# A sublayer's first products take the high part of input tile 0 alone, and the fillers of TensorE are seven at every sublayer

## The reference, cut to what matters

```python
for i in range(DEPTH):
    gn = norm_gains[i]
    h = h + 0.5 * rmsnorm(swiglu(rmsnorm(h, gn[0]), ffn1_w_in[i], ffn1_w_out[i]), gn[1])
    hn = rmsnorm(h, gn[2])
    ...                                  # m = the mixer of this layer on hn
    h = h + rmsnorm(m, gn[3])
    h = h + 0.5 * rmsnorm(swiglu(rmsnorm(h, gn[4]), ffn2_w_in[i], ffn2_w_out[i]), gn[5])
```

## Time and profile before

| | |
|---|---|
| median of 3 executions | 3162.06 us |
| the three executions | 3161.1, 3162.06, 3168.82 us |
| profiled execution, own time | 3175.51 us |
| its span, first to last instruction | 3173.4 us |
| granted TensorE clock, mean over the span | 0.996 |
| PE busy | 3125.5 us, 98% |
| DVE busy | 2176.7 us, 69% |
| ACT busy | 1666.1 us, 53% |
| DMA engines, mean share | 46.8%, 168 GB/s from HBM |

### The profile page before, as it was taken

One profiled execution on the slowest core, in us unless ns is written; L12 is line 12 of the kernel. 1 busy time (PEld: TensorE's weight loads), 2 busy tenths in 40 slices (PEclk: granted clock), 3 DMA queues, 4 the chain that ended last, 5 costly groups with the idle time before them and its releaser, 6 DMA issues.

```text
span 3173.4 us, 44497 instructions
## 1 busy us (share of the span) xinstructions
PE 3125.5 (98%) x17972; PEld 2719.3 (86%) x17972; DVE 2176.7 (69%) x2640; ACT 1666.1 (53%) x2064; POOL 4.0 (0%) x22
## 2 busy tenths in 40 slices
PE   9999999999999999999999999999999999999998
PEld 8888888888888888888888888888788888888887
DVE  7767675867586775675866777585874675857674
ACT  6565654645454654454546565454532554646553
POOL 0000000000000000000000000000000000000000
PEclk9999999999999999999999999999999999999999
DMA  6543454554355454455454345455432454554453
GB/s 231 186 172 130 151 186 173 186 187 158 120 186 186 173 186 172 147 186 186 173 186 170 123 159 186 166 193 187 149 143 107 156 186 163 199 186 149 151 191 120
DMA packets 75355, 534.77 MB, mean 169 GB/s; under 512 B 8480, under 2 KB 8608, under 8 KB 10784
## 3 DMA queue, kind: packets, MB, share of 16 engines
q1 hardware_dynamic: 75168, 532.07, 46.8%
HBM read 530.99 MB, written 1.05 MB: 168 GB/s over the span
## 4 chain that ended last, share of the span: by engine, by line
PE 93%; DVE 3%; ACT 1%; DVEq 1%; issue 1%; DMA 0%; SPq 0%; ACTq 0%
PE pp L2003 37%; PE pp L2004 18%; PE pm L2003 8%; PE pp L2153 5%; PE pm L2004 4%; PE pp L2026 4%; PE pp L2056 3%; PE pp L1998 2%; PE pp L1997 2%; PE pp L1999 2%; PE pp L2028 2%; PE pp L2196 1%; PE pm L1016 0%; PE pm L1029 0%; PE pp L373 0%
## 5 line engine op out<-in xcount | busy, mean ns | idle before, releaser
L2003 PE MATMUL pp<-xs,whi 128*128 128x512 f32 x4592 | 1628.8, 400 | 7.3 <-DVE tsum L1851 6.9
L1771 DVE TENSOR_TENSOR wlo<-raw,whi 128x2048 fp32r<-128x2048 f32 x453 | 1036.0, 2290 | 422.2 <-ACT whi L1575 421.7
L2004 PE MATMUL pp<-xs,wlo 128*128 128x256 f32 x4592 | 1288.6, 281 | 0.0
L2003 PEld LDWEIGHTS pp<-xs,whi 128*128 128x128 f32 x4592 | 864.3, 188 | 225.0 <-DVE tsum L1851 15.8
L1575 ACT ACTIVATE whi<-raw 128x2048 fp32r<-128x2048 f32 x453 | 864.3, 1911 | 281.8 <-DMA raw<-weights 280.8
L2004 PEld LDWEIGHTS pp<-xs,wlo 128*128 128x128 f32 x4592 | 869.7, 189 | 0.7
L1665 ACT ACTIVATE corr<-pp 128x512 f32<-128x512 f32 x335 | 199.3, 595 | 653.2 <-PE pp L2004 627.3
L1851 DVE TENSOR_TENSOR tsum<-pp,corr 128x512 f32<-128x512 f32 x323 | 222.8, 690 | 251.8 <-ACT corr L1665 251.6
L2003 PE MATMUL pm<-hs,whi 128*128 128x512 f32 x1056 | 377.3, 398 | 0.0
L2004 PE MATMUL pm<-hs,wlo 128*128 128x256 f32 x1056 | 297.0, 281 | 0.0
L2003 PEld LDWEIGHTS pm<-hs,whi 128*128 128x128 f32 x1056 | 199.1, 189 | 45.1
(11 more groups left out here) (346 smaller groups left out, 3133.6 us busy)
## 6 DMA issues: line engine op xcount, KB each, us to landing
raw<-weights SPq DMA_DIRECT2D x503, 1024.0 KB, 4.8
raw<-weights SPq DMA_DIRECT2D x8, 256.0 KB, 7.2
h<-x_by_feature SPq DMA_DIRECT2D x4, 256.0 KB, 6.7
out<-h SPq DMA_DIRECT2D x4, 256.0 KB, 2.5
vec<-vectors SPq DMA_DIRECT2D x1, 264.0 KB, 2.8
lamrow<-diff_lambda SPq DMA_DIRECT2D x1, 128.0 KB, 11.5
skiprow<-ssm_d SPq DMA_DIRECT2D x1, 8.0 KB, 12.3
```

Of the source, the lines that this page charges most:

```text
L1771: v.tensor_tensor(wlo[:, slot, :], raw[:, slot, :], whi[:, slot, :].bitcast(F32), ALU.subtract).then_inc(sem("weights_lo"), 1)
L2003: mm(bank, whi[:, slot, c:c + P], x_k, start=start, stop=False)
L2004: return mm(bank[:, 0:T], wlo[:, slot, c:c + P], x_k[:, 0:T], start=False, stop=stop)
```

## The change

`hi_of_tile_0` now posts a semaphore of its own, `x_hi_first`. In `rows`, tile 0 waits for that one, issues the four `wlo` products and then four `whi` products on the high part alone (256 columns each); only then it waits for the low part and issues four `whi` products on the low part alone (256 columns each, into the second half of the bank). The flag that opens the accumulation (`start`) moves to the `wlo` products of tile 0. Tiles 1 to 7 keep their order: `wlo` on the high part, then `whi` on both at once. The fillers are 7 ahead of every sublayer, where they were 5 ahead of all but the first.

```diff
             def hi_of_tile_0(s):
-                v.tensor_scalar(xs[:, 0, 0:T], h[:, 0, :], vec[:, 0, s["gain"]:s["gain"] + 1], None, ALU.mult)
+                v.tensor_scalar(xs[:, 0, 0:T], h[:, 0, :], vec[:, 0, s["gain"]:s["gain"] + 1], None, ALU.mult
+                                ).then_inc(sem("x_hi_first"), 1)
                 dve.drain()
...
                 def rows(k, outputs):
 
-                    for part in ("whi", "wlo") if k == 0 else ("wlo", "whi"):
-                        if part == "whi":
-                            pe.wait_ge(sem("x_lo"), KD * fill + k + 1)
-                        elif k:
-                            pe.wait_ge(sem("x_hi"), (KD - 1) * fill + k)
+
+
+                    if k:
+                        pe.wait_ge(sem("x_hi"), (KD - 1) * fill + k)
+                    else:
+                        pe.wait_ge(sem("x_hi_first"), fill + 1)
+                    for w in (wlo, whi) if k == 0 else (wlo,):
                         for half, ft in outputs:
-                            bank, slot, c = in_banks[half][:, ft, :], (g + half) % SLOTS, k * PC + ft * P
-                            if part == "whi":
-                                e = mm(bank, whi[:, slot, c:c + P], xs[:, k, :], start=(k == 0), stop=(k == KD - 1))
-                            else:
-                                e = mm(bank[:, 0:T], wlo[:, slot, c:c + P], xs[:, k, 0:T], start=False, stop=False)
+                            slot, c = (g + half) % SLOTS, k * PC + ft * P
+                            mm(in_banks[half][:, ft, 0:T], w[:, slot, c:c + P], xs[:, k, 0:T], start=(k == 0 and w is wlo), stop=False)
+                    pe.wait_ge(sem("x_lo"), KD * fill + k + 1)
+                    cols = slice(0 if k else T, 2 * T)
+                    for half, ft in outputs:
+                        slot, c = (g + half) % SLOTS, k * PC + ft * P
+                        e = mm(in_banks[half][:, ft, cols], whi[:, slot, c:c + P], xs[:, k, cols], start=False, stop=(k == KD - 1))
                     return e
...
             def first_of(s):
 
-                keep_clock(5 if s["n"] else 7)
+                keep_clock(7)
                 first_pair(s["segs"][0], s["fill"])
```

## The result

The changed kernel took 3166.59 us (median of 20 executions) beside 3162.08 us (20 executions) of the kernel before: a ratio of 1.0013, 95% interval 1.0008 to 1.0019. This is slower by 4.5 us. It lies inside the range of 3156 to 3169, but the interval leaves out "no change", which was the forecast. The executions spread from 3161.72 to 3175.27 us after and from 3157.43 to 3168.82 before. The spans of the two profiled executions, on the other hand, agree to 0.2 us (3173.4 before, 3173.2 after). Neither is a typical execution: 3175.51 us lies above all 20 of the kernel before, and 3175.27 is the longest of the 20 after.

What follows compares the result with a forecast made beforehand. PE, busy 98% of the span, was taken as the bound, with only 16.4 us of boundary waits to win. VectorE's later wait made each boundary's sum 0.00, so 3162 us stayed unchanged, range 3156 to 3169.

Steps and rivals of the forecast that it cites:

- What holds the boundary: At 17 boundaries VectorE's low part holds tile 1's `whi` group, so an earlier start of PE gains 0.00 us; chance 0.80.
- the bounds of -0.35 and +0.1: Limits per boundary in us: no later wait holds PE, or one more wait; times 17, -6.0 and +1.7 us.
- The early start: Rival at the boundaries: VectorE does not hold tile 1, gaining 17 x 0.35 = 6 us, to 3156; chance 0.07 (in part).
- Weight loads: Rival at tile 0: loads of 0.19 us don't hide, costing 14 us, to 3176; chance 0.04, shared with longer VectorE chain.
- The clock: Rival: longer fillers prevent half-clock drops at boundaries in unprofiled executions, saving 3 to 10 us, to 3152 to 3159; chance 0.05.
- the prediction's own sign: In the changed kernel's profile, a changed count or place of half-clock stretches would show the prediction wrong.
- A change of 0 carries over to the median unchanged: Whole kernel: the sum made on the profiled 3173.4 us, 13.5 above the median, applies to the median, giving 3162.
- 0, because the later wait is seen 17 times: At the 17 boundaries a later wait takes back PE's earlier start of 0.26 us, so the forecast gain is 0.
- R: Theory behind the experiments: executions differ in how many of 12 feed-forward sublayers run long; 4.5 us is about two more.
- F: Theory behind the experiments: the change has a fixed cost at each boundary, 4.5/17 = 0.26 us, unseen in the profiled execution.
- C: Theory behind the experiments: the stretches in which the granted clock is half have changed; ratio of 1.001 or more.

Runs made afterwards that it cites:

- entry256_split: Kernel before with only the split of tile 0 (5 fillers at 17 boundaries) and a 256-column filler ahead of panel 2: 3158.82 us, ratio 0.9957.
- entry256_fillers: Kernel before with only the 7 fillers at every boundary and a 256-column filler ahead of panel 2: 3158.43 us, ratio 0.9956.
- entry256_after: Changed kernel with a 256-column filler ahead of panel 2 in each feed-forward sublayer: 3158.55 us, ratio 0.9955 to the kernel before.

## Why the prediction was wrong, point by point

*What holds the boundary: right.* Every step of the sum at a boundary came out: 14 filler instructions in 3.19 us (about 3.2 said), PE's wait for the low part of tile 0 gone (under 2 us said), a new small wait for L1624 (the weight loads, 3.0 us in 17 places), PE's busy time up by 15.7 (some 14), and the `whi` group of tile 1 at 6.47 from the first filler (6.46) and 1.25 behind VectorE (1.25). The price of a boundary is -0.01 to +0.03 us, within the bounds of -0.35 and +0.1. The experiments with the rhythm settled agree in time: 0 to -1.6 us for the whole change.

*The rivals.* The early start did not come through: `entry256_split` is 0.4 us above `entry256_fillers`. Weight loads do hide: four products of tile 0 last 0.64 us, so (0.64 - 0.28)/3 = 0.12 a product as in the earlier trace rows, with a load of 0.19 us each. The rule on row groups from the Trainium skill (TensorE: Matmul & The Clock Gate, section The mechanism) disagrees with this trace as well. The clock: by the prediction's own sign a change in count or place of the half-clock stretches would count against it, and there are three before and four after, the new one in sublayer 16. But the new one is worth 1.5 us at most, all stretches lie inside mixers and none at a boundary, and traces of the changed kernel alone have from two to four. So the sign was no sign of the change.

*The step that failed* is the one with which the sum was carried over to the median: "The sum was made against the profiled execution, [...] which lies 13.5 above the median. A change of 0 carries over to the median unchanged". I named the 13.5 us and did not explain them. By the fitted line they are about seven sublayers of the long rhythm (13.5/1.97): the profiled execution has 9 long ones, and the median, 3160.0 us of span, would be near 2 ((3160.0 - 3155.7)/1.97). That is an estimate, for no execution of the kernel before near that median has a trace. Nor did I ask why the three executions differ by 7.7 us, other than for the clock. So the term that the sum put at nothing is the number of long sublayers, about 2 us each in 12 places. A kernel like this has no single time, and a forecast for it has to be one of odds. "0, because the later wait is seen 17 times" was right for the kernel's work and too narrow for its measured time. The measured +4.5 us are, by R, two sublayers more of the long rhythm. What the runs support is: the change has no cost of its own at the boundaries (shown by the 17 distances, and by `entry256_after` to within some 2 us); the time of a profiled execution follows the rhythms (shown in 20 traces); the 4.5 us of the first comparison are of that origin (inferred, by exclusion of F and C: only the slowest execution after has a trace, and it has one long sublayer fewer than that of before). Whether the change itself moved the odds, or the session did, stays open.

The evidence for two speeds was in the trace of before. Sublayers of equal instructions, some of 190.1 and some of 192.2 us, needed only a subtraction of the first fillers' starts.

## What to carry to other kernels

Before a small change is costed, compare the repeats of one stage inside one trace: equal instructions with unequal durations at the same clock and without idle time were here the sign of two rhythms, and the spread between executions was larger than the effect of the edit. Settle the rhythm first, here with a filler of 256 columns ahead of the wait from which PE runs without stopping (3158.6 us with a spread of 2.6 us, and 3160.2 with 3.7, against medians of 3162 to 3181 for both kernels), and measure edits on top of that. An early start gains nothing where PE soon meets a wait that another engine ends, as here the low part of tile 1. And an engine without idle time can still be held by another: compare its start with the end of the write that it waits for.

## What the hardware showed that was not expected

A stream of alternating products of 256 and 512 columns, each with its own weights, runs in one of two steady rhythms at the same full clock and the same busy share: 0.347 or 0.353 us a pair, 464 or 454 products in 80 us. The rhythm taken at the start holds over 110 us. The entries into the two differ by about 10 ns. A filler ahead of it of 128, 192 or 256 columns gave 0 and 3, 10 and 10, and 0, 1, 1, 0 and 1 long sublayers of 12. Entries that PE made 0.05 us behind VectorE's write went either way (119 long, 64 short), and those that its own filler held until 0.09 us behind it were short, 57 of 57. What inside the engine holds the two is not shown. The same program had medians of 3162, 3172, 3181, 3173, 3180, 3163 and 3175 us in seven sessions, while with the filler of 256 columns it had 3158.57 and 3160.15.
